# Attention in two passes: the turn of a token tile's reciprocal sums one step later

## What is computed

```python
def band_attend(q, k, v, q_pos, k_pos, rel_table):          # mixer A, 8 heads
    logits = einsum(q, k) * HEAD_DIM ** -0.5 + bias          # own chunk and 8 before it
    p = softmax(where(valid, logits, NEG))
    return einsum(p, v)

def dsa_attend(q, qi, wi, q_pos, k, v, ki, k_pos, t5_table, topk):   # mixer B, 8 heads
    # the top-k selection stands in a mask over all admissible keys
    logits = where(valid, einsum(q, ks) * HEAD_DIM ** -0.5 + bias, NEG)
    return einsum(softmax(logits), vs)

y = concatenate([oa, ob]) @ w_out
```

## Time and profile before

| | |
|---|---|
| time, median of three runs | 1787.72 us (1783.33 to 1788.44) |
| time of the profiled execution | 1786.2 us |
| span of its trace | 1784.4 us |
| first attention pass, in the trace | about 447 to 580 us |
| second attention pass, in the trace | about 580 to 920 us |
| PE busy, whole span | 89% |
| ACT, DVE, POOL busy, whole span | 35%, 40%, 5% |

### The profile page before, as it was taken

The page is one execution under the profiler, slowest core; times in us unless marked ns, Lnnn a source line. Parts: engine busy times, 40 slices in busy tenths (PEclk is TensorE's granted clock), DMA queues, the critical chain, the costliest instruction groups (busy, mean ns, idle before and its releaser), DMA issues. The chain is left out here.

```text
span 1784.4 us, 25603 instructions
## 1 busy us (share of the span) xinstructions
PE 1586.2 (89%) x10329; PEld 1381.9 (77%) x10329; DVE 709.5 (40%) x1388; ACT 631.6 (35%) x1184; POOL 92.7 (5%) x120
## 2 busy tenths in 40 slices
PE   4799988898799888998955999999999998999994
PEld 2578778898488445655515999999999998999993
DVE  3514677679354443442214111111111113444446
ACT  5424458771466343442215111111111113333332
POOL 2202000000000011110020000000000000000001
PEclk9899999999699799998687999999999998999997
DMA  9567013120400510000013111111111106000005
GB/s 356 191 227 240 13 33 99 51 46 3 154 2 2 145 45 27 24 25 24 15 54 106 47 47 47 47 47 43 40 46 47 47 12 259 1 1 0 0 0 221
DMA packets 100846, 126.38 MB, mean 71 GB/s; under 512 B 15896, under 2 KB 82520, under 8 KB 97408
## 3 DMA queue, kind: packets, MB, share of 16 engines
q1 hardware_dynamic: 95664, 108.98, 18.6%
q0 software_dynamic: 5104, 16.34, 2.6%
HBM read 111.17 MB, written 20.54 MB: 74 GB/s over the span
## 5 line engine op out<-in xcount | busy, mean ns | idle before, releaser
L1421 PE MATMUL ps<-h_hi,gu_hi 128*128 128x352 f32 x1056 | 341.7, 324 | 8.9 <-DVE gu_lo L1457 8.9
L1421 PE MATMUL ps<-h_lo,gu_hi 128*128 128x352 f32 x1056 | 339.3, 321 | 0.0
L1421 PE MATMUL ps<-h_hi,gu_lo 128*128 128x352 f32 x1056 | 339.0, 321 | 0.0
L1421 PEld LDWEIGHTS ps<-h_hi,gu_hi 128*128 128x128 f32 x1056 | 198.9, 188 | 9.0 <-DVE gu_lo L1457 9.0
L653 PE MATMUL ps<-x_hi,w_hi 128*128 128x352 f32 (+1 forms) x552 | 189.1, 343 | 12.8 <-POOL x_lo L505 8.4
L1421 PEld LDWEIGHTS ps<-h_lo,gu_hi 128*128 128x128 f32 x1056 | 199.2, 189 | 0.0
L1421 PEld LDWEIGHTS ps<-h_hi,gu_lo 128*128 128x128 f32 x1056 | 198.6, 188 | 0.0
L1510 PE MATMUL ps<-a_hi,wd_hi 128*128 128x352 f32 x528 | 174.2, 330 | 13.9 <-DVE a_lo L1533 13.9
L653 PE MATMUL ps<-x_lo,w_hi 128*128 128x352 f32 (+1 forms) x552 | 181.2, 328 | 0.0
L653 PE MATMUL ps<-x_hi,w_lo 128*128 128x352 f32 (+1 forms) x552 | 181.2, 328 | 0.0
L1510 PE MATMUL ps<-a_lo,wd_hi 128*128 128x352 f32 x528 | 172.1, 326 | 0.0
(11 more groups left out here) (211 smaller groups left out, 2389.6 us busy)
## 6 DMA issues: line engine op xcount, KB each, us to landing
upper<-in_w_ada SPq DMA_DIRECT2D x16, 1024.0 KB, 4.6
gate_raw<-in_w_gate SPq DMA_DIRECT2D x22, 512.0 KB, 3.7
up_raw<-in_w_up SPq DMA_DIRECT2D x22, 512.0 KB, 3.7
lower<-in_w_in SPq DMA_DIRECT2D x18, 512.0 KB, 5.1
lower<-in_w_ada SPq DMA_DIRECT2D x8, 1024.0 KB, 22.8
hidden<-scratch_y SPq DMA_DIRECT2D x4, 2048.0 KB, 12.5
w_down_all<-in_w_down SPq DMA_DIRECT2D x3, 2560.0 KB, 23.0
upper<-in_x_prompt SPq DMA_DIRECT2D x4, 1024.0 KB, 8.9
```

Of the source, the lines that this page charges most:

```text
L1421: mm = nc.tensor.matmul(B(3 * i + c, CH), cut[i][a][:, P * k:P * k + P], h[:, NTOK * k + CH * c:NTOK * k + CH * (c + 1)], start=(k == 0 an ...
```

## The change

The R item of tile t moves from the end of step 4t + 5 to step 4t + 6. There it stands behind the first group of T items, which belong to pair 4t + 4, the first pair of tile t + 1, and ahead of the P items that finish tile t. For the last tile, which has no next tile, it stands ahead of its last P items in the step after the last T items. Nothing is added or removed, and the reciprocals on DVE and the spread on POOL stay where they are.

```diff
--- before.py
+++ after.py
@@ -148,11 +148,12 @@
             blocks = -(-width(pairs[u][0]) // P)
             for group in groups_of(blocks):
                 items += [("T", u, b, nb) for b, nb in group]
+                if u and u % PAIRS == 0 and group[0][0] == 0:
+                    items.append(("R", u // PAIRS - 1))
                 items += [("P", *it) for it in pending]
                 pending = [(u, b, nb) for b, nb in group]
-            if u % PAIRS == PAIRS - 1:
-                items.append(("R", u // PAIRS))
         elif pending:
+            items.append(("R", NT - 1))
             items += [("P", *it) for it in pending]
             pending = []
```

## The result

The changed kernel took 1764.51 us, the median of four runs (1762.92 to 1768.58), against 1788.08 us for the kernel before (four runs, 1783.33 to 1789.26). A second comparison with more runs gave 1767.64 us against 1786.6, ratio 0.9893 (0.9872 to 0.9914), or 19 us. The profiled execution of the changed kernel took 1762.92 us, its span is 1761.1.

The account below looks back on a forecast made before the run. PE, busy 89% of the span, was taken as the bound, holding ready work behind R's wait for DVE and POOL. Second pass 8.9 plus first pass 2.4 gave 11.3 us gained, about 1775 us; range 1768.5 to 1783.5.

Parts of the forecast that it names:

- the sum: Both passes: 8.9 us from the second plus 2.4 us from the first, 11.3 us gained, about 1775 us.
- rival (b): Second pass: PE holds its higher clock longer; 1.7 us more behind tile 6, 0.5 in tile 0; 1772.5 us; chance 0.10.
- The gap ahead of R, 10.5 us in tiles 1 to 6: Second pass, step 4t + 5: W starts earlier by 7.76 us of R's waits plus 2.76 us of R's own time.
- The price in step 4t + 6: Second pass, R's new place: tiles 1 and 2 nothing, 3 and 4 0.8 us each, 5 0.5, 6 0.1.
- What was late next: Second pass: DVE's masks in tiles 1 and 2, its P-released multiply in 3 and 4, ACT's copy of R in 5.
- Tile 0 of the second pass, 1.1 us: At the low clock: next QK 1.9 us earlier, R costs 1.0 us a step later, 0.21 of it in idle time.
- First pass, 2.4 us: R's four waits for POOL, 2.5 us, go; new waits near nothing, bounded by 0.1 each in tiles 3 to 7.
- The rest of the second pass, forecast to lose 0.6 us: Tiles 6 to 8: tile 6 loses 0.1 us, tile 7 0.5 at a partly low clock, tile 8 nothing.
- (a) The ring binds: Second pass, tiles 3 to 6: R takes one of three banks ahead of P; gain 5 to 8, about 1779.5 us; chance 0.17.
- (c): Second pass: ACT's late copy of R delays DVE's final multiply and next masks in every tile; about 1788.5 us; chance 0.03.
- (d): No gain: the gap ahead of R only moves, to ring banks and DVE's masks ahead of QK; 1786 us; chance 0.06.
- upper bound of gain, 15.3 us: Whole change: R's new waits cost nothing in tiles 3 to 7 and 0; 11.3 + 1.6 + 0.5 + 0.1 + 1.0 + 0.8.

Follow-up runs that it names:

- the kernel with tile 0 alone: Kernel before, with R moved to its new place for tile 0 of the first pass only; 1783.34 us in one execution.

## Why the prediction was wrong, step by step

**The step that failed** is the sum, which held the granted clock of every stretch as the trace of before has it and left what the clock may bring to rival (b), sized at 2.2 us (1.7 behind tile 6, 0.5 in tile 0). The order brought some 12 us, about the 11.3 that were forecast; the clock brought some 7 us more: 2.8 in the first pass, 0.5 in tile 0 of the second and some 4 behind tile 5.

**The gap ahead of R, 10.5 us in tiles 1 to 6: right.** The W halves of the changed kernel's second profile against the third of the kernel before come earlier, tile after tile, by 2.3, 2.1, 2.0, 1.8, 1.6 and 1.2 us more at the place where R stood, 11.0 in sum. From the first W half to the last W of tile 5 the granted clock is 1.00 in both, so this is order alone.

**The price in step 4t + 6: right in kind, small in size.** Read at the next W half, tiles 1 and 2 lose 0.1 us each (forecast 0), tiles 3 and 4 lose 1.1 and 1.0 (0.8 each), tile 5 loses 0.6 (0.5). The sum is 2.9 for 2.1. What was late next was as named: DVE's multiply, released by P, and in tile 5 by ACT's copy of R.

**Tile 0 of the second pass, 1.1 us: right, and the clock adds 0.5.** The first W half comes 1.8 us earlier (24.8 us behind the pass's first QK, the mean of six profiles of the old order, against 23.0). The order has 1.3 of that: the QK of pair 7 comes 17.95 us behind the first QK in place of 19.20. The rest is the clock, which rises 19.0 to 20.2 us behind the first QK in the seven profiles of the new order and 23.0 to 24.9 us behind it in five of the six of the old one (18.8 in the sixth); it is the 0.5 that rival (b) had there. In all, the last W of tile 5 comes 9.8 us earlier (207.1 on average against 197.3), 9.3 of them by order, where the terms of the prediction up to there give 10.5 + 1.1 - 2.1 = 9.5.

**First pass, 2.4 us: the order is a little more, 3.0, and the whole is 5.8.** With tile 0 at the new place in both, the changed kernel takes 33.7 us from the QK of pair 9 to that of pair 20 and the kernel with tile 0 alone 36.0, 2.3 less; with 0.7 for tile 0 that is 3.0. The mean of the whole pass is 132.9 us in seven profiles of the old order and 127.2 in five of the new. Of the other 2.8 us some 1.5 are the earlier rise, and 1.3 the end of the pass: the clock falls there in all profiles, 114.5 to 119.0 us behind QK of pair 1, and by then the new order is all but through: its second pass begins at 116.1 to 116.4, that of the old order at 120.3 to 123.2. The prediction looked at no clock in the first pass at all.

**The rest of the second pass, forecast to lose 0.6 us (tile 6's 0.1 and tile 7's 0.5): it gains 3.8 on average.** R itself costs some 0.2 us there, by the length of the rest times its clock (106.5 and 106.7, above); the other 4 us are the clock. Rival (b) was right that the clock falls less, and right in its place in part: the fall behind tile 6's idle is in four of six profiles of the old order and in none of the new, and is worth the 1.7 us that it had for it. It was short in two ways. These four have more falls, and the mean gain is more than twice as large; and the idle does not bring the fall by itself, since two profiles have the idle and a granted clock of 1.00 behind it. Where the falls come in these 130 us differs between executions of one program. Why the new order has the long version less often stays open; its earlier place in time, or its fewer idles, would both do it, and no run here tells them apart.

The Trainium skill, "TensorE: Matmul & The Clock Gate", section "A second HAM failure mode: psum-queue depth-cycling", which stood beside rival (b), lets small idles between groups of matmuls bring the falls. Tile 6's two kinds of window, 0.66 and 1.00 behind the same idle, show that one such idle is not enough here. The same page of the Trainium skill, section "What's actually happening", says that the chip's look at the activity runs freely and does not begin with the kernel, so that one kernel changes its clock at different points; the 18.6, 20.0 and 20.5 us of the three profiles of the kernel before agree.

**The sum of what was measured:** by stretches 5.8 + 9.8 + 3.8 = 19.4 us, as in the second comparison (19 us); the order has 3.0 + 9.3 - 0.2 = 12.1 of it, against 11.3 forecast (2.4 + 9.5 - 0.6), and the clock 7.3. The first comparison's 22 us, and the 23.3 us between the two profiles first seen, hold some luck: the projection ahead of the first QK took 446.7 us in the one and 445.0 in the other, and 132.2 and 125.1 us are the two ends of the rest of the pass.

**The other rivals.** (a) The ring binds: no. Its banks cost 2.9 us of waits of R in tiles 3 and 4, and moving R one or two T items up takes 2.2 us of that back without any more banks. (c) No: of the 18 tiles' ends in both passes the final multiply waits for ACT's copy of R in two, 0.7 us in sum. (d) No: the waits of QK for the masks are 14.7 us where the kernel before has 16.2, and 13.9 in its second profile, so the gap did not move there. The reason that the Trainium skill, "Perfetto Trace Analysis", section "Optimization Strategy", names for such gaps is not the one here: with the same three banks the gap is gone, so it was not a lack of buffers.

**The chances.** The side was right. The range missed because its upper bound of gain, 15.3 us, was made of waits and order alone. Rival (b), given 0.10, named the right cause; the reason held against it, that gaps of 1.5 us elsewhere leave the clock up, was true of those places and did not carry over to others.

## What to carry to other kernels

Where an in-order engine waits for a chain that has only just begun, put ready work in between, and look for the place whose own operand or buffer is not the next one late: here 11.0 us were to be had in tiles 1 to 6, 2.9 went to the new place, and a place one item earlier gives 2.2 of it back. When waits of the matmul engine are removed from a stretch that is partly at its low clock, don't hold the clock of the old trace in the sum: give the clock a term of its own, in every stretch where the granted clock is under 1, and widen the range by what two profiles of the unchanged kernel differ there. Take several profiles of one program before a cause is read out of one fall of the clock.

## What the runs showed of the hardware that was not expected

One program differs by 7 us in a stretch of 130 us with the same work, the same waits and the same order, by the granted clock alone (0.79 and 0.84 over 120 us). The part of all 14 profiles ahead of the first QK, which no edit touches, took from 444.9 to 451.3 us. The same wait of 1.3 us of PE was followed by 5 us at a granted clock of 0.66 in four executions, and of 1.00 in two.
